# A two-layer transformer block on one core: residuals, squares and output by halves of 512 columns, tile 0 normalised on ScalarE, the gate's broadcast moved ahead of the transposes

## The reference

```python
for l in range(DEPTH):                                   # DEPTH = 2
    mod = jnp.einsum('bd,de->be', cond, w_ada[l]) + b_ada[l]
    sh1, sc1, g1, sh2, sc2, g2, sh3, sc3, g3 = [m[:, None, :] for m in jnp.split(mod, N_MOD, axis=-1)]
    h = modulate(rms_norm(x, norm_ffn1[l]), sh1, sc1)
    x = x + 0.5 * g1 * swiglu(h, w_gate1[l], w_up1[l], w_down1[l])
    h = modulate(rms_norm(x, norm_mix[l]), sh2, sc2)
    x = x + g2 * token_mixing(h, w_in[l], ...)
    h = modulate(rms_norm(x, norm_ffn2[l]), sh3, sc3)
    x = x + 0.5 * g3 * swiglu(h, w_gate2[l], w_up2[l], w_down2[l])
```

## Time and profile before

| | |
|---|---|
| median of 3 runs | 1177.69 us (1175.96, 1177.69, 1180.74) |
| profiled execution, own time | 1175.71 us |
| its span, first to last instruction | 1174.0 us |
| PE busy | 1137.6 us (97%) |
| DVE busy | 864.6 us (74%) |
| ACT busy | 530.6 us (45%) |
| mean granted TensorE clock | 0.995 of full speed |

### The profile page before, as it was taken

The page is one execution under the profiler, slowest core; times in us unless marked ns, Lnnn a source line. Parts: engine busy times, 40 slices in busy tenths (PEclk is TensorE's granted clock), DMA queues, the critical chain, the costliest instruction groups (busy, mean ns, idle before and its releaser), DMA issues.

```text
span 1174.0 us, 20341 instructions
## 1 busy us (share of the span) xinstructions
PE 1137.6 (97%) x7924; PEld 1023.1 (87%) x7924; DVE 864.6 (74%) x1263; ACT 530.6 (45%) x685; POOL 64.7 (6%) x79
## 2 busy tenths in 40 slices
PE   6999999998999999999999999999999999999998
PEld 3699999988898799999988999998989877999997
DVE  5788788797866877766778887888887588645545
ACT  3334433553556543443363344336456545433432
POOL 2101110100000000000001011100000000000000
PEclk9999999999999999999999999999999999999999
DMA  9899889944511667678747988894842155666461
GB/s 304 278 339 315 296 300 329 319 143 150 180 55 54 216 215 250 229 238 266 261 159 244 338 300 296 300 361 148 254 143 88 58 172 167 204 210 196 161 196 72
DMA packets 160371, 258.41 MB, mean 220 GB/s; under 512 B 8365, under 2 KB 127277, under 8 KB 160319
## 3 DMA queue, kind: packets, MB, share of 16 engines
q1 hardware_dynamic: 140739, 182.25, 46.9%
q0 software_dynamic: 19584, 75.50, 19.1%
HBM read 256.56 MB, written 1.05 MB: 219 GB/s over the span
## 4 chain that ended last, share of the span: by engine, by line
PE 78%; DVE 12%; ACT 3%; DVEq 2%; DMA 2%; issue 2%; SPq 0%; ACTq 0%
PE bank L1246 23%; PE bank L1248 23%; PE bank L1247 23%; DVE wlo L854 4%; PE bank L1587 2%; DVE room L796 2%; PE bank L1506 2%; DVE acc L796 1%; DVEq L798 1%; ACT whi L458 1%; DMA xs<-in_x_dram 1%; DMA ada<-in_w_ada_dram 1%; PE bank L1491 1%; PE bank L1568 1%; DVE xn L955 1%
## 5 line engine op out<-in xcount | busy, mean ns | idle before, releaser
L1246 PE MATMUL bank<-hhi,whi 128*128 128x256 f32 (+1 forms) x1600 | 454.6, 284 | 0.0
L1248 PE MATMUL bank<-hhi,wlo 128*128 128x256 f32 (+1 forms) x1600 | 452.6, 283 | 0.0
L1247 PE MATMUL bank<-hlo,whi 128*128 128x256 f32 (+1 forms) x1600 | 452.5, 283 | 0.0
L458 ACT ACTIVATE whi<-raw 128x2048 fp32r<-128x2048 f32 (+1 forms) x174 | 321.6, 1851 | 10.4 <-PE bank L1695 5.3
L1246 PEld LDWEIGHTS bank<-hhi,whi 128*128 128x128 f32 (+1 forms) x1600 | 306.1, 191 | 4.1 <-issue 2.0
L1247 PEld LDWEIGHTS bank<-hlo,whi 128*128 128x128 f32 (+1 forms) x1600 | 306.1, 191 | 2.4 <-issue 0.5
L1248 PEld LDWEIGHTS bank<-hhi,wlo 128*128 128x128 f32 (+1 forms) x1600 | 306.1, 191 | 0.0
L854 DVE TENSOR_TENSOR wlo<-raw,whi 128x2048 fp32r<-128x2048 f32 (+2 forms) x130 | 281.5, 2197 | 20.5 <-ACT whi L458 19.9
L796 DVE SCALAR_TENSOR_TENSOR room<-ada,cT,room 128x512 f32 (+3 forms) x266 | 170.0, 639 | 22.0 <-issue 2.6
L510 ACT ACTIVATE eb<-bank 128x512 f32<-128x512 f32 x40 | 23.9, 597 | 338.6 <-PE bank L1248 338.6
L972 DVE TENSOR_TENSOR wlo<-raw,whi 128x1024 fp32r<-128x1024 f32 x44 | 53.9, 1226 | 134.0 <-ACT whi L458 133.0
(11 more groups left out here) (218 smaller groups left out, 1150.6 us busy)
## 6 DMA issues: line engine op xcount, KB each, us to landing
ada<-in_w_ada_dram POOLq DMA_DIRECT2D x68, 1024.0 KB, 6.4
raw<-in_w_gate_dram SPq DMA_DIRECT2D x44, 1024.0 KB, 6.1
raw<-in_w_up_dram SPq DMA_DIRECT2D x44, 1024.0 KB, 6.8
raw<-in_w_down_dram SPq DMA_DIRECT2D x44, 1024.0 KB, 5.5
raw<-in_w_in_dram SPq DMA_DIRECT2D x28, 1024.0 KB, 6.0
raw<-in_w_out_dram SPq DMA_DIRECT2D x8, 512.0 KB, 3.3
raw<-in_w_out_dram SPq DMA_DIRECT2D x4, 1024.0 KB, 5.8
room<-in_w_ada_dram POOLq DMA_DIRECT2D x3, 1024.0 KB, 14.0
```

The costliest lines, as they stand in the source:

```text
L458: last = act.activation(dst, src, ACT.Copy)
L1246: pe.matmul(ps, l_hi, r_hi, start=first, stop=False)
L1247: pe.matmul(ps, l_hi, r_lo, start=False, stop=False)
L1248: return pe.matmul(ps, l_lo, r_hi, start=False, stop=last)
```

## The change

Five things are done:

- `residual` multiplies and adds by halves of 512 columns and signals `x_ready` at each half. `split_lo(0)` no longer stands between the tiles at n = 2 but behind `high_of_h`, as at n = 0 and 1.
- ACT squares by halves; the first half's sum becomes the bias (`ev`) of the Ln over the second. DVE's correction has one step more (`refine_halves`).
- Tile 0 is scaled into `xn` on ACT, in two copies that stand behind tile 1's Exp.
- At n = 1 the gate's first broadcast stands ahead of all transposes. `keep_running` stands ahead of them too: 8, 6, 17 products at n = 0, 1, 2 (before 0, 0, 14), and no longer 3 between the tiles at n = 0 and 2.
- The output is stored by four DMAs of half a tile, not two of a tile.

```diff
             for t in range(TT):
-                sp.wait_ge(x_ready, NB * TT * L + t + 1)
-                sp.dma_start(out_v[:, t, :], xs[:, t, :]).then_inc(x_out, 16)
+                for h, (a, b) in enumerate(HALVES):
+                    sp.wait_ge(x_ready, ((NB * L - 1) * TT + t) * 2 + h + 1)
+                    sp.dma_start(out_v[:, t, a:b], xs[:, t, a:b]).then_inc(x_out, 16)
...
                 for t in range(TT):
-                    act.wait_ge(x_ready, x_done + t + 1)
-                    act.activation(xn[:, t, :], xs[:, t, :], ACT.Square, accum_out=ss[:, t, 0:1])
-                    root(t)
+                    for h, (a, b) in enumerate(HALVES):
+                        act.wait_ge(x_ready, (turned(l, n) * TT + t) * 2 + h + 1)
+                        act.activation(xn[:, t, a:b], xs[:, t, a:b], ACT.Square, accum_out=ss[:, t, h:h + 1])
+                        if h == 0:
+                            act.drain().then_inc(ss_half, 1)
+                            act.activation(ev[:, t:t + 1], ss[:, t, 0:1], ACT.Identity, scale=1.0 / D, bias=eps[:, :])
+                    act.drain().then_inc(ss_ready, 1)
+                    act.activation(rs[:, t, 0:1], ss[:, t, 1:2], ACT.Ln, scale=1.0 / D, bias=ev[:, t:t + 1])
+                    act.drain()
+                    act.activation(rs[:, t, 0:1], rs[:, t, 0:1], ACT.Exp, scale=-0.5).then_inc(rs_ready, 1)
...
+                act.wait_ge(q_ready, turned(l, n) + 1)
+                for a, b in HALVES:
+                    act.activation(xn[:, 0, a:b], xs[:, 0, a:b], ACT.Copy, scale=tn[:, 0, 0:1]).then_inc(xn_act, 1)
...
+            def refine_halves(l, n, t):
+                v, r, q = (w[:, t, 0:1] for w in (var, rs, tn))
+                dve.wait_ge(ss_half, turned(l, n) * TT + t + 1)
+                dve.tensor_scalar(v, ss[:, t, 0:1], -0.5 / D, -0.5 * EPS, ALU.mult, ALU.add)
+                dve.drain()
+                dve.wait_ge(ss_ready, nth(l, NN, n * TT + t + 1))
+                dve.scalar_tensor_tensor(v, ss[:, t, 1:2], -0.5 / D, v, ALU.mult, ALU.add)
+                dve.drain()
+                dve.wait_ge(rs_ready, nth(l, NN, n * TT + t + 1))
+                dve.scalar_tensor_tensor(q, r, r, v, ALU.mult, ALU.mult)
+                dve.drain()
+                last = dve.scalar_tensor_tensor(q, q, 1.5, r, ALU.add, ALU.mult)
+                if t == 0:
+                    last.then_inc(q_ready, 1)
+                else:
+                    dve.drain()
+                    for a, b in HALVES:
+                        dve.tensor_scalar(xn[:, t, a:b], xs[:, t, a:b], q, None, ALU.mult).then_inc(xn_dve, 1)
...
                 high_of_h(l, n)
-                if n < 2:
-                    split_lo(0, use)
+                split_lo(0, use)
                 low_of_h(l, n)
...
-                    if n == 1 and t == 1:
-                        split_lo(0, turn(l, U_FFN[1]))
...
             def turn_h(l, n):
-                if n == 2:
-                    keep_running(PS[7], 14)
+                if n == 1:
+                    pe.wait_ge(x_ready, turned(l, n) * TT * 2 + 3)
+                    spread_gate(l, 1, 0)
+                    keep_running(PS[7], 6)
+                else:
+                    keep_running(PS[7], (8, 0, 17)[n])
                 for t in range(TT):
                     for k in range(KT):
...
-                    if n == 1:
-                        spread_gate(l, 1, t)
-                    else:
-                        keep_running(PS[7], (3, 5)[t])
+                if n == 1:
+                    spread_gate(l, 1, 1)
+                else:
+                    keep_running(PS[7], 5)
```

More of the change, by code:

```diff
@@ L140, in build @@
         eps = sb("eps", [P, 1])
+        ev = sb("ev", [P, TT])
         heads = room[:, 0:16, :]
@@ L218, in build @@
         xn_ready = sem("xn_ready")
+        ss_half = sem("ss_half")
+        q_ready = sem("q_ready")
+        xn_act = sem("xn_act")
+        xn_dve = sem("xn_dve")
         tp_done = sem("tp_done")
@@ L331, in build, with turned @@
         NN = NB * TT
+        HALVES = ((0, HALF), (HALF, D))
+        def turned(l, n):
+            return l * NB + n - 1
         Y_PARTS = [("C", 0), ("C", 1), ("AB", 0), ("AB", 1)]
@@ L466, in root, with boundary @@
                 act.activation(rs[:, t, 0:1], rs[:, t, 0:1], ACT.Exp, scale=-0.5).then_inc(rs_ready, 1)
-            def boundary(l, n, x_done):
+            def boundary(l, n):
                 for t in range(TT):
-                    act.wait_ge(x_ready, x_done + t + 1)
-                    act.activation(xn[:, t, :], xs[:, t, :], ACT.Square, accum_out=ss[:, t, 0:1])
-                    root(t)
+                    for h, (a, b) in enumerate(HALVES):
[8 more added lines that the diff above has]
+                    act.activation(rs[:, t, 0:1], rs[:, t, 0:1], ACT.Exp, scale=-0.5).then_inc(rs_ready, 1)
                     if n == 2 and t == 0:
@@ L672, in _ @@
                 if l > 0:
-                    boundary(l, 0, nth(l, NB * TT, 0))
+                    boundary(l, 0)
                 ffn(l, 0, U_IN)
-                boundary(l, 1, nth(l, NB * TT, TT))
+                boundary(l, 1)
                 for n in range(NC + 1):
@@ L731, in _ @@
                 split_hi(0, turn(l, U_FFN[1]))
-                boundary(l, 2, nth(l, NB * TT, 2 * TT))
+                boundary(l, 2)
                 ffn(l, 1, U_LAYER if l + 1 < L else None)
@@ L746, in _ @@
                 dve.memset(heads1[k * HD:(k + 1) * HD, k * HD:(k + 1) * HD], 1.0)
-            dve.sem_inc(x_ready, TT)
             dve.wait_ge(iotas, 3)
@@ L932, in boundary @@
             def boundary(l, n, use):
-                refine(l, n, 0)
+                refine_halves(l, n, 0)
                 if n < 2:
                     modulation(l, n, PS[6][:, 0:2 * KT])
-                refine(l, n, 1)
+                refine_halves(l, n, 1)
                 high_of_h(l, n)
-                if n < 2:
-                    split_lo(0, use)
+                split_lo(0, use)
                 low_of_h(l, n)
@@ L955, in residual @@
                         dve.tensor_tensor(xn[:, t, cut], DB[2 * t + half][:, :], gate[:, cut], ALU.mult)
-                    dve.drain()
-                    if n == 1:
-                        dve.tensor_tensor(xs[:, t, :], xs[:, t, :], xn[:, t, :], ALU.add).then_inc(x_ready, 1)
-                    else:
-                        dve.scalar_tensor_tensor(xs[:, t, :], xn[:, t, :], 0.5, xs[:, t, :], ALU.mult, ALU.add).then_inc(x_ready, 1)
+                        dve.drain()
+                        if n == 1:
+                            dve.tensor_tensor(xs[:, t, cut], xs[:, t, cut], xn[:, t, cut], ALU.add).then_inc(x_ready, 1)
+                        else:
+                            dve.scalar_tensor_tensor(xs[:, t, cut], xn[:, t, cut], 0.5, xs[:, t, cut], ALU.mult, ALU.add).then_inc(x_ready, 1)
             def ffn_step(l, which, i, ahead, after, weighs=True):
@@ L1332, in turn_h @@
                         if k % 4 == 0:
-                            pe.wait_ge(xn_ready, nth(l, 2 * NN, (n * TT + t) * 2 + k // 4 + 1))
+                            pe.wait_ge((xn_act, xn_dve)[t], turned(l, n) * 2 + k // 4 + 1)
                         at_ = (k % 2) * S + t * P
```

2 lines of the change are left out of this document (1 added, 1 removed).

## The result

The changed kernel takes 1185.37 us in the median of 20 runs (1178.78 to 1189.2). The kernel before, run beside it, takes 1180.7 (1174.64 to 1184.38, 20 runs). The ratio is 1.004 [1.0023, 1.0058], so it is 4.7 us slower. The forecast was 2.96 slower, and 1179.8 in all.

What follows compares the result with a forecast made beforehand. The chain was 78% PE and 12% DVE; DVE set most boundaries before, PE's queue would decide n = 0 and 1 after. 2.1 + 0.64 + 0.74 - 0.52 = +2.96 us on 1176.8 gave 1179.8, range 1175.3 to 1183.

Steps and rivals of the forecast that it cites:

- the four terms: Boundaries n = 1 +2.1 for two layers, n = 0 +0.64, n = 2 +0.74 for two, output -0.52 us.
- the moved split: At n = 2, the weight split between hhi and hlo on DVE: +0.75 us per boundary, with nothing absorbing it.
- What the prediction named to look for: Trace signs: PE not idle at n = 1, ACT's copies releasing PE at n = 2, wlo waiting for DVE, 2.1 us last DMA.
- its marks in time at n = 0 and 1: Tile 1's transposes 6.6 us after the sums' start at n = 1; tile 0's 1.7 behind the sums' end at n = 0.
- estimate of 3.2 us for a 512 KB store: At the output, from the skill's fixed DMA cost of about 2 us: 3.2 us, where the trace has 2.7.
- The term of the sum: At the output, half-tile stores save 0.64 us and the later addition costs 0.12: -0.52.
- The four times of before, 1175.71 to 1180.74, have 1176.8 in their middle; I add the sum to that: Base for the whole kernel: 1176.8 us, to which +2.96 is added, giving 1179.8.
- A zero product costs 0.216: On PE at the boundaries: 0.216 us per zero product, since fourteen take 3.19 and three 0.81.
- Rival C: PE's gaps at all five boundaries bring the clock down: +8, with the sum +11, 1188 us; chance 0.05.
- If PE's clock falls at a boundary: One of the prediction's signs that it is wrong, at any boundary.
- Rival A: Zero products hide behind late copies or roots at n = 0 and 1: +0.5, or 1177.3 us; chance 0.18.
- Rival B: Boundaries get shorter through halves and DVE's relief, output 0.5 less: -5.0, or 1171.8 us; chance 0.10.

Runs made afterwards that it cites:

- g3: Changed kernel with each column sum's product 128 columns wide, not 1; 1178.62 us, ratio to before 0.9993.
- i1: Changed kernel with 128-column sums and zero products added in two other long waits of PE; 1177.31 us, ratio to before 0.9977.
- g1: Kernel before, unchanged, run again for a second profile and each run's clock; 1181.64 us, ratio to before 1.0012.
- e4: Kernel before with only 8 and 6 zero products added ahead of the transposes at n = 0 and 1; 1184.11 us, ratio 1.0049.
- g4: Changed kernel without 8 and 6 zero products at n = 0 and 1, n = 2 split back between tiles, 128-column sums; 1176.97 us, ratio 0.9979.
- h3: Kernel before with 128-column sums and without any zero product at the boundaries; 1176.72 us, ratio to before 0.9958.
- e3: Changed kernel without 8 and 6 zero products at n = 0 and 1, n = 2 split back between tiles; 1180.78 us, ratio to before 1.0011.
- g2: Kernel before with each column sum's product 128 columns wide, not 1; 1177.49 us, ratio to before 0.9981.
- h4: Changed kernel, 128-column sums, no zero products at n = 0 and 1, tile 0 scaled on DVE, zero products in two long PE waits; 1176.52 us, ratio 0.9963.

## Why the prediction was wrong

The direction was right; the time lay outside the range of 1175.3 to 1183 by 2.4 us. Its steps, one by one:

**The sum of the four terms was right.** g3 and i1 have the changed order without a fall at a boundary. g3 is laid beside the first trace of before here; i1 gives the same to 0.04 us:

| place | before | g3 | measured | forecast |
|---|---|---|---|---|
| n = 1, sums' start to first `hhi` (layer 0) | 6.42 | 7.46 | +1.04 (layer 1: +1.05) | +1.06 |
| n = 0, the same | 6.41 | 7.03 | +0.62 | +0.64 |
| n = 2, first zero product to the next FFN's broadcast, layer 0 | 193.31 | 193.94 | +0.63 | +0.37 |
| the same, layer 1 | 193.68 | 193.88 | +0.20 | +0.37 |
| first broadcast of the output's end to the span's end (changed kernel) | 12.6 | 12.1 | -0.5 | -0.52 |

At n = 2 `hhi` starts 0.15 (layer 0) and 0.58 (layer 1) earlier than before, and the moved split then costs 0.78 in both; forecast were 0.38 and 0.75. The layers differ because before `hhi` came 0.38 later in layer 1 (7.54 behind the first zero product, against 7.16), which the forecast, read from layer 0 alone, didn't have. That one miss makes good for the other (0.83 for 0.74) is luck.

Together 2·1.05 + 0.62 + 0.83 - 0.5 = +3.05, forecast +2.96. What the prediction named to look for is there too: no idle time of PE at n = 1, ACT's copies as releaser at n = 2, 0.86 of waiting for DVE's `wlo`, stores in 2.0 to 2.1. Only its marks in time at n = 0 and 1 fail in the changed kernel's own trace, by the clock: tile 0's transposes stand 3.4 us behind the sums (614.85 against 611.48), not 1.7.

The prediction's estimate of 3.2 us for a 512 KB store rests on a fixed cost that the Trainium skill ("DMA: Bandwidth & Descriptors", section "Anatomy of one DMA") gives for DMAs issued by GpSimd. These stores are issued by SP, and took 2.7 at 512 KB and 2.0 to 2.1 at 256 KB. The term of the sum came from the rows and holds.

**The first step that failed: "The four times of before, 1175.71 to 1180.74, have 1176.8 in their middle; I add the sum to that".** Twenty runs of before have a median of 1180.7, and 108 more in the four sets have medians of 1179.9 to 1181.2. So the base was 3.9 too low, of the 5.6 us missed; with 1180.7 the forecast would have been 1183.7. Behind it stands a reading of the profile: a mean clock of 0.995 was taken as the kernel's, where it is the lucky end. Of those 108, the ten runs at 0.994 to 0.995 took 1174.7 to 1177.4, while 40 of the 44 at 0.986 to 0.988 took 1180 to 1187; their mean clock is 0.989.

**The second: "A zero product costs 0.216".** It does at the full clock. In the changed kernel's profile the clock falls at the one-column sums directly ahead, at all three boundaries that have them, and then one costs 0.43 (0.46 on average at n = 1 of layer 1, whose broadcast takes 2.05 in place of 1.02), on PE's queue, which now decides. From sums' start to `hhi` the changed kernel's trace is 1.7, 3.2 and 3.3 us longer at those three than g3's. Where g1 has such falls, against the first trace of before, it pays 1.4 and 2.4 (7.80 and 8.83 against 6.42 and 6.41). The difference, with falls in most profiles, fits the 1.7 us by which +4.7 exceeds +2.96. The runs point the same way: at a mean clock of 0.994 the changed kernel's median is 1179.0 (5 runs) and that of before 1175.2 (6 of the 108), 3.8 apart; at 0.988 they are 1187.3 (6) and 1181.1 (18), 6.2 apart. These runs are few and not side by side, and 2.96 us is a ratio of 1.0025, inside the interval [1.0023, 1.0058], so the excess is likely and not proven. What is shown is that zero products alone slow the kernel before as much as the change does (e4), that they cost 2.1 of the 3.05 us at full clock (g3, g4), and that without the falls the changed kernel takes 1178.6 or 1177.3 (g3, i1).

**Rival C** had the right resource and the wrong place. It said that the clock decides "once PE stands still at n = 2 beyond what it did before" and that the gap at n = 0 and 1 is gone. PE did not stand still there, and the falls came there all the same. "If PE's clock falls at a boundary" stood among what would make me wrong, and that happened. The sentence that the trace shows such a fall "once, and none at a boundary" was a misreading in its first half. Besides the fall that the prediction shows, the trace of before has two behind waits of PE, outside the boundaries (windows of before, same columns as above):

```profile
270.00:272.00 2.00, 0.78 (x7) 0.77 (x8) 1.79 (x4) 0.70 (x1) 0.00 (x0) 1.00 1.10 351
272.00:276.00 4.00, 4.00 (x29) 3.76 (x29) 3.92 (x5) 1.09 (x2) 0.00 (x0) 0.57 0.46 123
625.00:627.00 2.00, 0.39 (x2) 0.35 (x3) 1.52 (x4) 1.32 (x2) 1.28 (x2) 1.00 0.42 111
627.00:631.00 4.00, 4.00 (x12) 3.17 (x11) 3.52 (x4) 3.12 (x3) 0.00 (x0) 0.57 0.94 316
```

Its second half was true of that execution only. The Trainium skill's "TensorE: Matmul & The Clock Gate", section "Why this matters for your kernels", speaks of idle gaps between bursts; h3's rows at n = 2 agree (0.39 busy in 3.00 us, then 0.50), but the falls at n = 0 and 1 don't follow a gap.

**Rival A** (the zero products hide) is refuted by e4, by g3 against g4 and by the idle 3.27 us of DVE. **Rival B** (shorter boundaries) is refuted by the table above, and not only by PE's queue: at n = 0 and 1 DVE's pass over tile 1 is not earlier (241.93 - 236.93 = 5.00 behind the sums' start, before 4.96), since it stands behind the modulation, which waits for the sums, and g4, without the zero products, is still longer there than before. Only at n = 2 and at the output did the halves bring anything. What the parts of the change are worth without the zero products, e3 and g4 show: nothing measurable against before and g2.

**Open** stays why the same program has a fall at a given place in one execution and not in another, and how much of the 4.7 us is the dearer price of a fall. Only widths of 1 and 128 columns were run, so nothing here says which width between them would do.

## What to carry to other kernels

Filler for the clock belongs where the engine waits anyway; once its queue is what ends last, each further filler is paid in full, and twice if the clock is down. Before the base of a forecast is fixed, look at the time and granted clock of many runs, not at one good profile: here runs of the same kernel lay 10 us apart, more than the change moved it. And when a fall of the clock follows busy rows, look at how wide those products are, since widening them can be nearly free.

## What the hardware showed that I had not expected

- One-column products keep PE at 100% busy in the profile and are still followed by half the clock: seen at the sums of the changed kernel (240.8, 609.4) and of before (605.9 in g1), in 17 of 21 places. At 128 columns the 32 of them took 3.74 us instead of 3.63, and no fall stands at the 27 places in nine profiles.
- Each fall in the profiles, but for those cut off by the end, held the clock at 0.50 for long enough to take about 1.7 or about 3.4 us of full-speed time from PE. By span and mean clock the profile of before lost 5.4 us in this way, that of the changed kernel 13.65, of g1 13.1, of h4 1.7. Not all of it is paid in the kernel's time, since part falls into waits.
- A fall does not always cost what it takes from PE. h3 runs at 0.990 against g2's 0.994 and is no slower by its runs; in its trace each fall at n = 2 takes 3.4 us of full-speed time, and `hhi` comes 0.7 later: part of the fall lies in PE's wait.
